# First chunk's loads on the two hardware DMA queues, input weights issued at once, and new planner costs and priorities in a hybrid decoder layer

## What is computed

```python
h = rmsnorm(x, norm_mix_pre)                       # stage A
q, k, v, lx, lg = split(h @ w_in)                  # stage B: 1792 columns; conv of width 4 on lx
lru = rg_lru(causal_dwconv(lx)) * gelu(lg)         # stage D: gates, associative scan over positions
attn = sliding_window_attention(q, k, v, sinks)    # stage C: 128-query blocks, window 128, ALiBi, sinks
y = concat(rmsnorm(attn), rmsnorm(lru)) @ w_out    # stages N and E
x = x + rmsnorm(y, norm_mix_post)                  # stage E
f = causal_dwconv(rmsnorm(x, norm_ffn_pre) @ w_up) # stages F and U: 5632 columns, conv of width 3
x = x + rmsnorm((gelu(gate) * val) @ w_down, norm_ffn_post)   # stage G
```

## Time and profile before

| | |
|---|---|
| time, median of 3 runs | 731.14 us (730.08 to 731.97) |
| profiled execution, its span | 729.0 us, on the slowest of 8 cores (724.2 to 729.0) |
| PE busy | 686.2 us, 94% |
| DVE, ACT, POOL busy | 439.5, 385.2, 322.5 us |
| table loads on ACT | 19, 24.4 us together |
| DMA moved | 77.62 MB, mean 106 GB/s |

### The profile page before, as it was taken

The page is one execution under the profiler, slowest core; times in us unless marked ns, Lnnn a source line. Parts: engine busy times, 40 slices in busy tenths (PEclk is TensorE's granted clock), DMA queues, the critical chain, the costliest instruction groups (busy, mean ns, idle before and its releaser), DMA issues.

```text
span 729.0 us, 10728 instructions; the slowest of 8 cores (724.2 to 729.0 us)
## 1 busy us (share of the span) xinstructions
PE 686.2 (94%) x3689; PEld 319.9 (44%) x3689; DVE 439.5 (60%) x474; ACT 385.2 (53%) x540; POOL 322.5 (44%) x426
## 2 busy tenths in 40 slices
PE   6889789888997998999999999999999999999996
PEld 2644334443443444444444444444444444444442
DVE  3766958966976667877777721115777777751112
ACT  4587989789599466645545511114454554531112
POOL 7142876854722654555645421113445445431111
PEclk9999999999999999999999999999999999999999
DMA  8967477526208558778999634345534444303334
GB/s 162 214 166 243 119 169 162 148 59 145 87 2 147 110 121 187 129 117 134 142 149 155 114 57 51 45 56 82 87 64 80 87 91 84 59 1 50 52 48 83
DMA packets 32871, 77.62 MB, mean 106 GB/s; under 512 B 11441, under 2 KB 11569, under 8 KB 32818
## 3 DMA queue, kind: packets, MB, share of 16 engines
q0 software_dynamic: 16992, 52.17, 44.5%
q1 hardware_dynamic: 15232, 23.95, 10.9%
q10 hardware_dynamic: 594, 0.82, 0.5%
HBM read 88.72 MB, written 18.87 MB: 148 GB/s over the span
## 4 chain that ended last, share of the span: by engine, by line
PE 74%; POOL 6%; DMA 6%; issue 6%; DVE 5%; ACT 2%; DVEq 0%; POOLq 0%; ACTq 0%; SPq 0%
PE ps L540 73%; DMA win<-w_in_r 2%; POOL stats L513 2%; DMA ye_104<-w_out_r 1%; POOL stats L510 1%; DMA ye_105<-x 1%; PE ps L545 1%; DMA ye_103<-w_out_r 1%; DVE ye_103 L520 1%; DMA xt_78<-x 1%; POOL wob L510 0%; DVE xcb_71 L513 0%; POOL xt_79 L513 0%; DVE thx_114 L513 0%; DVE ct_86 L520 0%
## 5 line engine op out<-in xcount | busy, mean ns | idle before, releaser
L520 DVE SCALAR_TENSOR_TENSOR T_124<-ps,pp,T_124 128x1023 f32<-128x1023 f32 x88 | 112.7, 1281 | 36.7 <-ACT T_124 L500 17.6
L520 DVE SCALAR_TENSOR_TENSOR T_125<-ps,pp,T_125 128x1023 f32<-128x1023 f32 x88 | 112.8, 1282 | 34.5 <-ACT T_125 L500 16.9
L500 ACT ACTIVATE T_124<-ps,pp 128x1024 f32<-128x1024 f32 x44 | 53.0, 1204 | 71.4 <-PE ps L540 71.4
L500 ACT ACTIVATE T_125<-ps,pp 128x1024 f32<-128x1024 f32 x44 | 52.9, 1203 | 68.5 <-PE ps L540 68.5
L510 POOL TENSOR_SCALAR stats<-stats 128x1 f32<-128x1 f32 (+1 forms) x68 | 25.0, 368 | 119.5 <-ACT yf_174 L500 17.4
L540 PE MATMUL ps<-hT_76,win 128*128 128x512 bf16 (+1 forms) x248 | 51.9, 362 | 4.0 <-DMA win<-w_in_r 2.2
L540 PE MATMUL ps<-hT_77,win 128*128 128x512 bf16 x208 | 49.4, 380 | 2.6 <-DVE stats L510 1.0
L513 POOL TENSOR_TENSOR stats<-stats,nhalf 128x1 f32<-128x1 f32 (+1 forms) x63 | 45.7, 727 | 7.2 <-POOL stats L510 0.2
L540 PEld LDWEIGHTS ps<-hT_76,win 128*128 128x128 bf16 x248 | 24.6, 102 | 25.5 <-issue 7.6
L540 PE MATMUL ps<-wob,lruT 128*128 128x512 bf16 x128 | 30.8, 384 | 2.4 <-DVE ye_105 L520 1.0
L540 PE MATMUL ps<-h2T_63,wu_121 128*128 128x512 bf16 x128 | 30.2, 379 | 0.5 <-DVE ye_103 L520 0.5
(11 more groups left out here) (409 smaller groups left out, 1502.5 us busy)
## 6 DMA issues: line engine op xcount, KB each, us to landing
wu_121<-w_up_r POOLq DMA_DIRECT2D x15, 512.0 KB, 7.6
wu_122<-w_up_r POOLq DMA_DIRECT2D x15, 512.0 KB, 7.5
wu_123<-w_up_r POOLq DMA_DIRECT2D x14, 512.0 KB, 6.3
win<-w_in_r POOLq DMA_DIRECT2D x14, 256.0 KB, 20.8
ye_103<-x POOLq DMA_DIRECT2D x7, 512.0 KB, 6.5
ye_104<-x POOLq DMA_DIRECT2D x6, 512.0 KB, 6.4
out<-ye_103 SPq DMA_DIRECT2D x6, 512.0 KB, 5.1
out<-ye_104 SPq DMA_DIRECT2D x5, 512.0 KB, 4.3
```

The costliest lines, as they stand in the source:

```text
L500: return e.activation(**kw)
L520: return P.op({"dve": (dur, lambda e: e.scalar_tensor_tensor(out=_v(out), in0=_v(in0), scalar=scalar, in1=_v(in1), op0=op0, op1=op1), lock ...
```

## The change

At the start of the program:

- x of chunk 0: tile 0 goes half on SP's and half on ACT's queue, tile 1 on SP's, tile 2 on ACT's, tile 3 on SP's, each of the last three as one transfer.
- `g0bc` is loaded by one DMA of 512 KB on ACT's queue (128 copies of the row lie in DRAM); `gain_row`, `grow` and `onef` go.
- W_in, `wabx` and chunk 1's x wait on POOL for the identity (made on POOL itself) instead of tile 0.
- The x loads of chunks 2 and 3 wait for the last W_in block.
- 22 warming products in place of 9.

In the planner: `BW` is 420e3; 524288 bytes are booked for a W_in or w_down transfer; `LAT` is a table by pair of engines, `BACK` lets an engine's next instruction start a little earlier, `DLAT` gives each queue a lead and a trail; `LX` and `LS` are no longer read. `TUNE["J"]` has 142 offsets instead of 34, and operations outside any stage now have the offset "none" = -12.8. The stage bases stay. What each stage computes stays, too.

```diff
-        "TRA": ..., "WD": [5, 0.6], "WARM": 9, "HALF": 5,
+        "TRA": ..., "WD": [5, 0.6], "WARM": 22, "HALF": 5,
-        "J": {"N1.2": -60, "F3.3": -68, ... }}
+        "J": {"A0": -3.1, "A0.0": -23.6, ..., "B3.0": 29.3, "B3.1": 169.9, ..., "B3.5": 384.7, ...,
+              "E3.2": -312.1, ..., "F2.1": -558.1, ..., "N2.3": -406.4, ..., "none": -12.8}}
...
-BW = 323e3
+BW = 420e3
-LAT = {"pe": 0.12, "act": 0.15, "dve": 0.12, "pool": 0.20, "sp": 0.1}
+LAT = {"pe": {"pe": 0.0, "act": 0.26, "dve": 0.27, "pool": 0.32, "sp": 0.3},
+       "act": {"pe": 0.2, "act": 0.09, "dve": 0.1, "pool": 0.17, "sp": 0.1},
+       "dve": {"pe": 0.15, "act": 0.1, "dve": 0.08, "pool": 0.145, "sp": 0.07},
+       "pool": {"pe": 0.15, "act": 0.095, "dve": 0.105, "pool": 0.12, "sp": 0.07}}
+BACK = {"pe": 0.0, "act": 0.1, "dve": 0.04, "pool": -0.08, "sp": 0.0}
+DLAT = {"sp": (0.9, 1.35), "act": (0.9, 1.35), "pool": (1.7, 1.35)}
...
-                f = p.fin
-                if p.is_dma:
-                    f += 0.1
-                elif p.eng != e:
-                    f += LAT[p.eng]
-                elif e != "pe":
-                    f += 0.06
+                f = p.fin + (0.1 if p.is_dma else LAT[p.eng][e])
...
+            if o.is_dma and e == "pool" and t > 0:
+                t += 0.5
...
-                x0 = max(issue + 0.8, bus[q])
-                need = o.nbytes / BW * (TUNE["LS"] if x0 > 30 else 1.0)
+                lead, trail = DLAT[e]
+                x0 = max(issue + lead, bus[q])
+                need = o.nbytes / BW
...
-                o.fin = bus[q] + 1.3 + (TUNE["LX"] if o.slot[0] in ("xa", "x1o") else 0.0)
+                o.fin = bus[q] + (0.0 if o.is_store else trail)
...
-    XQ = {0: ("sp", -101), 1: ("act", -101), 2: ("pool", -49.6), 3: ("pool", -49.5)}
+    XQ = {0: ("sp", "act"), 1: ("sp",), 2: ("act",), 3: ("sp",)}
...
-    dma("act", grow[:], gr_d[0:1, 0, :], 4096, [], ["grow"], -120, "c6")
-    P.op({"dve": (0.1, lambda e: e.memset(onef[:], 1.0))}, [], ["onef"], -120)
+    dma("act", g0bc[:], gr_d[:, 0, :], 524288, [], ["g0bc"], -101.5, "c6")
...
-            dma("pool", win[:, fc, :, :], win_d[fc], 613000, [xbuf(0, 0)[1]], [("win", fc)], -50 + n,
-                ("win", fc))
+            dma("pool", win[:, fc, :, :], win_d[fc], 524288, ["ident"], [("win", fc)], -50 + n, ("win", fc))
...
-        dma("pool", wabx[:], wabx_d[:, :, :], 524288, [xbuf(0, 0)[1]], ["wabx"], -45.5, "c3")
+        dma("pool", wabx[:], wabx_d[:, :, :], 524288, ["ident"], ["wabx"], -45.5, "c3")
...
-    def gain_row():
...
-        if k == 0 and tl < 2:
-            for h, rs in enumerate((slice(0, 64), slice(64, 128))):
-                dma(XQ[tl][0], X[rs, :], x_d[t * 128 + rs.start:t * 128 + rs.stop, :], 262144, [], [xk + "b" * h],
-                    XQ[tl][1] + 0.1 * h, xk + "b" * h)
-        elif k == 0:
-            dma("pool", X[:], rows, 524288, [xbuf(0, 0)[1]], [xk], XQ[tl][1], xk)
+        if k == 0:
+            n = len(XQ[tl])
+            for h, q in enumerate(XQ[tl]):
+                rs = slice(h * 128 // n, (h + 1) * 128 // n)
+                dma(q, X[rs, :], x_d[t * 128 + rs.start:t * 128 + rs.stop, :], 524288 // n, [], [xk + "b" * h],
+                    -102 + tl, xk + "b" * h)
         elif k == 1:
-            dma("pool", X[:], rows, 524288, [xbuf(0, 0)[1]], [xk], -40.5 + 0.1 * tl, xk)
+            dma("pool", X[:], rows, 524288, ["ident"], [xk], -40.5 + 0.1 * tl, xk)
         else:
-            dma("sp", X[:], rows, 524288, [], [xk], KA[k] + tl - 30, xk)
+            dma("sp", X[:], rows, 524288, [("win", 13)], [xk], KA[k] + tl - 30, xk)
...
-    gain_row()
...
-                        dma("pool", wdn[i][:], wdn_d[:, i, :], 613000, ["uT%d" % cpi], ["wdn%d" % i],
+                        dma("pool", wdn[i][:], wdn_d[:, i, :], 524288, ["uT%d" % cpi], ["wdn%d" % i],
```

More of the change, by code:

```diff
@@ L21 @@
         "KC": [22, 2, 171, 154], "KE": [15, 170, 329, 3], "FK": 550, "VCAP": 2, "HYS": 20.0, "PEN": 0.3,
[L22 removed]
+        "TRA": [0, 0, 1, 1], "TRE": [0, 0, 0, 0], "NA": [0, 0, 0, 1], "WD": [5, 0.6], "WARM": 22, "HALF": 5,
         "SE": 3, "SD": 9, "SC": 3.5, "CN": 22.0, "SA": 1, "SB": 6.5, "SPB": 4, "SPU": 4, "SWP": 0.0,
         "LX": 4.0, "LS": 1.0,
[L25 removed]
[20 rows of a table added]
 ENGS = ("pe", "act", "dve", "pool", "sp")
[L28 removed]
+BW = 420e3
 TABSETS = {"G": "gelu_apprx_tanh_and_others", "L": "natural_log_exp_and_others"}
[L30 removed]
+LAT = {"pe": {"pe": 0.0, "act": 0.26, "dve": 0.27, "pool": 0.32, "sp": 0.3},
[4 more added lines that the diff above has]
+DLAT = {"sp": (0.9, 1.35), "act": (0.9, 1.35), "pool": (1.7, 1.35)}
 def _v(x):
@@ L51, in __init__ @@
         self.deps, self.groups = set(), []
-        self.is_dma, self.slot, self.nbytes = False, None, 0
+        self.is_dma, self.is_store, self.slot, self.nbytes = False, False, None, 0
         self.eng, self.done, self.tload = None, False, None
@@ L64, in __init__ @@
         self.ng = 0
-        self.stg = self.sub = None
+        self.stg, self.sub = None, "none"
     def group(self, nb):
@@ L98, in op @@
             o.is_dma, o.nbytes, o.slot = True, dma, slot
+            o.is_store = slot[0] in ("x1o", "xoo") or slot[:-1] in ("scraw", "screw")
         lw, rd = self.lw, self.rd
@@ L355, in schedule @@
                     bus[oq] += ov / 2
-                o.fin = bus[q] + 1.3 + (TUNE["LX"] if o.slot[0] in ("xa", "x1o") else 0.0)
+                o.fin = bus[q] + (0.0 if o.is_store else trail)
             else:
                 o.fin = st + dur
-                free[e] = o.fin
+                free[e] = o.fin - BACK[e]
                 if locked(o, e):
@@ L366, in schedule @@
                         vheld[0] -= g.nb
-                    tend = max([ops[i].fin + LAT[ops[i].eng] for i in g.members if ops[i].eng != "pe"], default=0.0)
+                    tend = max([ops[i].fin + LAT[ops[i].eng]["pe"] for i in g.members if ops[i].eng != "pe"], default=0.0)
                     for x in range(g.bank, g.bank + g.nb):
@@ L609, in build_nc @@
     L0 = cur[0]
-    grow = P.tile("grow", [1, D], F32, L0)
-    onef = P.tile("onef", [1, 128], F32, L0 + 12288)
     bbase = P.tile("bbase", [128, 2, 128], F32, L0 + 13312)
@@ L821, in stage_a @@
             X, xk = xbuf(k, tl)
-            xk = [xk, xk + "b"] if k == 0 and tl < 2 else [xk]
+            xk = [xk + "b" * h for h in range(len(XQ[tl]))] if k == 0 else [xk]
             na = TUNE["NA"][k]
```

## The result

The changed kernel takes 727.46 us (725.35 to 727.80) against 730.76 for the kernel before, measured beside it: a ratio of 0.9947 [0.993, 0.9964]. It is faster, by 3.3 us where 11 were forecast.

The account below looks back on a forecast made before the run. PE was taken to bound the feed-forward part, with gains made before it. 729.0 - 2 (start) - 9 (order) = 718.0 us of span, plus 2.1 gives 720.1 us timed; range 706 to 734.

Parts of the forecast that it names:

- What bounds the kernel: Feed-forward part, last 304 us, is unbroken and bound by PE; gains or losses made before it count in full.
- The order: New planned order fills PE's gaps before the feed-forward part: 9 us gained, 11.3 located, bounds 0 to -20.
- The start's first product: PE's first W_in product, at 15.91 before, was to move by 0, bounds -2.0 to +3.2.
- Warming: At the start, 22 products take 9.8 us, ending before the first transpose; value 0, 1.6 us kept for the range.
- W_in: At the start, earlier block transfers remove PE's two waits for W_in: -2.2 us, bounds -0.9 to -3.6.
- the start's sum: First product, W_in waits and warming together: 0 - 2.2 + 0, rounded to -2 us, bounds +2.3 to -7.2.
- x behind the last W_in block: On SP's queue, an early chunk 2 x load now stands behind the last W_in block; costed at nothing.
- loads booked too fast: Rival: plan runs up to 14.2 us ahead of W_in loads, streams stall, order gives half; 738.8 us, chance 0.16.
- C: Experiments' theory about the start: loads come later than the plan books them, and streams stop; 13 to 16 us idle expected.

Follow-up runs that it names:

- f_less_win: Changed kernel, planned order kept, last four W_in blocks set to zero on VectorE instead of loaded, output wrong in the gated part; 721.66 us, 0.9884.
- f_x_before_g: Changed kernel, planned order kept, tile 0's second half sent before g0bc on ACT's queue; 726.85 us, 0.9953.
- f_warm42: Changed kernel, planned order kept, 42 warming products instead of 22; 725.90 us, 0.9939.
- f_x_early: Changed kernel, planned order kept, chunk 2's first two x loads issued before the last W_in block instead of waiting for it; 729.61 us, 0.9984.
- plan_only: Kernel before with only the changed kernel's planner numbers, offsets and booked bytes, its start operations kept; 759.93 us, 1.0396.
- book_slow: Changed kernel replanned with transfers before 45 us booked at 285 GB/s instead of 420, offsets kept; 745.83 us, 1.0208.
- refit: Changed kernel with transfers booked at 285 GB/s before 45 us and 300 before 75, offsets searched anew; 735.0 us, 1.0058.
- f_w_mid: Changed kernel, SP's loads reordered, chunk 2's squares and sums moved back, w_out block writes placed by traced landing times; 724.16 us, 0.9921.

## Why the prediction was right or wrong

**What bounds the kernel: right.** The feed-forward part is an unbroken run as in the earlier trace rows (287.50 us from 432.09, and 84.61 from 329.26), and f_less_win's 5.8 us earlier restart became 5.8 us at the end by the medians, 4.6 by the ratios.

**The order: right in sign and place, in size partly by luck.** 9 us were taken near a located 11.3; idle PE from 80 to 300 fell by 11.4. But of the 11.3 only 7.6 had been located in that stretch (3.7 lay between 45 and 53.5), and a part of the 7.6 was clock and not idle time; so at least 3.8 us of the gain came from gaps that the prediction had not named. The low clocks of the earlier trace rows are gone, and U0's products are spread over the attention's last work: the first stands at 243.74, and 48.94 us without a gap follow from 266.44. Idle PE from 60 to 240 was forecast near 13; it is 16.3, of which 4.2 lie before 80.

**The start's first product: inside its bounds.** Forecast 15.91 with -2.0 to +3.2; it is at 17.44. The first square starts at 9.68, where 250 GB/s gave 9.3. The rule of the Trainium skill ("DMA: Bandwidth & Descriptors", "Rules for kernel authors") that spreading transfers over the queues brings no bandwidth fits the traces: from 3 to 45 us the loads moved 206 GB/s before and 206 after. What moved x was its place in a queue: f_x_before_g brought it forward by 3.7 us on the same queues, and the time stayed.

**Warming: the working was wrong, the value of 0 right.** 22 products were to take 9.8 us, at the 0.44 of each of the nine before; they took 6.32, since later ones are faster (the 20 that f_warm42 adds take 0.24 each), and they end 4.95 us before the first transpose. f_warm42 closes that gap and wins 1.4 us, near the 1.6 kept for it in the range, but by luck: the 1.6 were to come from two groups of products, and the first of them still takes 1.86 us. The loads take the 1.4 back, as the prediction said.

**W_in: the transfers as forecast, the gain not.** The last block lands at 44.6 in place of 47.5, 2.9 us earlier, within 0.9 to 3.6. The value of -2.2 for PE's waits failed: they are 2.4 us. That the blocks land earlier doesn't help streams that were planned for 33.

**The step that failed** is the start's sum, -2 us (bounds +2.3 to -7.2), and in it the sentence on x behind the last W_in block: "I cost it at nothing". The chain of waits shows a price there. f_x_early shows that the edge was not the mistake: without it the same bytes come in another order and the restart stays. The mistake was to price the start by what the loads do, and the order by what the old gaps were, as if the two did not meet. The new order asks for x at 40 and `w_out`'s first two blocks at 43 and 44, where the chip has x at 54 and writes these blocks from 58.3 and 59.5. Measured by idle PE before 80 us, the term is +10.5, over four times its upper bound; plan_only has most of it without the new loads, and book_slow gets 6.3 of it back by the booking alone.

**The rival "loads booked too fast" named this mechanism,** with the right cause (1.25 us booked for a W_in block; the 19 transfers on GpSimd's queue took (44.6 - 2.87) / 19 = 2.2) and a stall of up to 14.2 us. Two things in it failed. What was held against it, that PE asks for W_in hardly faster than it comes, is true of W_in (one wait, 2.38 us); the stall falls on the loads behind W_in, x and `w_out`, which ask at once for what the burst has delayed. And it was set up as another world, with half the order's gain, when both happened: the middle's full gain and the start's stall. The ledger of the result is the sum with both terms: 729.0 + 10.5 - 11.4 - 0.3 - 1.6 = 726.2, the span.

**Open.** refit's start is as C expected, and its plan still ends 27 us ahead of the chip, as the changed kernel's does by 30.5 (plan 695.7), while the kernel before was 15.3 behind its own (713.7). What the rest of that distance consists of, no run here took apart.

## What to carry to other kernels

Set the plan's landing times beside the trace's: where an order written ahead of time expects a load 10 us before it lands, a gain elsewhere can be paid for at that load, and in a full burst moving that load forward made the next one late. Give each in-order stream its waits in the order in which the loads land, and look at who frees the buffer of each of them: writes put off until the work on chunk 1 or chunk 2's x was done stopped other engines for 7 to 11 us. And when one change brings a located gain and a located risk in different stretches, forecast their sum, not one or the other.

## What the runs showed of the hardware

While PE stood idle at the stops near 55 to 60 us, the granted clock went to its lower level, and it stayed there when PE was busy again. The stretch 60 to 70 of the changed kernel (columns as in the earlier trace rows):

```profile
60.00:70.00 10.00, 5.77 (x28) 2.00 (x28) 8.56 (x13) 7.93 (x14) 6.02 (x11) 0.50 0.80 259
```

The clock reads 1.00 from 56 to 58, during the stop of 5.95 us, and 0.50 (1.2 GHz) from 60 on; it is back at 1.00 from 73. Two products on `xcb`, `wabx` took 0.59 us at 38.07 and 1.16 at 67.67. In f_w_mid, where PE's longest stop there is 3.15 us, the stretch 60 to 70 stands at 0.50 as well, with PE busy 7.13 of 10 us, and the clock is back at its upper level only from 77. These stops are thus paid for twice, and a shorter stop did not bring the higher level back sooner.
